# Attention groups of a two-block transformer: one pipeline slot in another order

## The reference

```python
# block 1 (_mixing): three kinds of heads
oa = _dsa(qa, ka, va, qi, ki, wi)       # 4 heads, top-128 keys of an index score
ob = _stick_breaking(qb, kb, vb)        # 4 heads
oc = _swa_sinks(qc, kc, vc, sinks)      # 8 heads, window of 128 keys, a sink each
o = jnp.concatenate([oa, ob, oc], axis=2)
o = _rms(o, g_out).reshape(B, L, MIX_WIDTH)      # root mean square of each head's output
return o @ w_o
...
# block 2 (_hybrid_mixer)
p = _masked_softmax(s1, mask) - lam * _masked_softmax(s2, mask)   # _diff_attention, 4 heads
...
o = _rmsnorm(o, subln_g, SUBLN_EPS) * (1.0 - lambda_init)
...
p = _masked_softmax(sc, _chunk_mask(start, s))   # _mla, 4 heads, no norm behind it
...
return jnp.concatenate([y_a, y_b, y_c], axis=-1) @ w_out          # y_c: a state space scan
```

## Time and profile before

| | |
|---|---|
| median of 3 runs | 3133.03 us (3124.57 to 3137.35) |
| the profiled execution | 3130.37 us, span 3128.6 us, mean granted clock of PE 0.951 |
| PE busy in the span | 2908.3 us (93%) |
| DVE busy | 1787.2 us (57%) |
| ACT busy | 756.2 us (24%) |
| POOL busy | 931.1 us (30%) |

### The profile page before, as it was taken

How to read it: one execution, slowest core, us unless ns; L and a number is a source line. 1 busy time by engine, 2 the same in 40 slices (tenths; PEclk the granted TensorE clock), 3 DMA queues, 4 the chain that set the end, 5 groups by cost and what they waited for, 6 DMA issues and landing times.

```text
span 3128.6 us, 33693 instructions
## 1 busy us (share of the span) xinstructions
PE 2908.3 (93%) x12126; PEld 2133.1 (68%) x12126; DVE 1787.2 (57%) x3803; ACT 756.2 (24%) x1781; POOL 931.1 (30%) x794
## 2 busy tenths in 40 slices
PE   8888999999997899999989988999999998899997
PEld 4354688888544578888854456888884454688886
DVE  2673469388367447938854545877824634551433
ACT  2354310000235431000022353201112335320111
POOL 0301224443330124444412202344440400344442
PEclk9989999999998799999989988999999998899998
DMA  6115034244221013434421101254421210122221
GB/s 256 64 61 215 28 138 166 101 148 170 91 80 61 1 55 121 175 108 156 154 76 56 61 27 68 108 183 186 156 100 57 59 50 23 40 94 96 81 81 54
DMA packets 45412, 313.28 MB, mean 100 GB/s; under 512 B 5424, under 2 KB 5552, under 8 KB 31040
## 3 DMA queue, kind: packets, MB, share of 16 engines
q1 hardware_dynamic: 42912, 306.88, 27.0%
q10 hardware_dynamic: 2304, 4.20, 0.6%
q0 software_dynamic: 32, 0.07, 0.0%
HBM read 298.53 MB, written 2.10 MB: 96 GB/s over the span
## 4 chain that ended last, share of the span: by engine, by line
PE 70%; DVE 18%; ACT 6%; issue 3%; DMA 1%; POOL 1%; DVEq 0%; SPq 0%; ACTq 0%; POOLq 0%
PE bank L1114 39%; PE bank L1094 9%; PE bank L1440 7%; PE bank L1168 3%; DVE nw L2067 3%; PE bank L1264 2%; DVE sel L2304 2%; DVE m L2303 1%; PE bank L1307 1%; DVE SPT L2368 1%; ACT SPT L1756 1%; PE bank L1294 1%; PE bank L1229 1%; PE bank L1567 1%; DMA sel<-in_mod_pieces 1%
## 5 line engine op out<-in xcount | busy, mean ns | idle before, releaser
L1000 POOL TENSOR_TENSOR SPT<-ring 128x512 f32<-128x512 f32 (+2 forms) x140 | 175.2, 1252 | 956.3 <-DMA ring<-in_slabs 493.0
L1114 PE MATMUL bank<-U,ring 128*128 128x256 f32 x1728 | 412.2, 384 | 10.8 <-DVE U L2101 10.5
L1114 PEld LDWEIGHTS bank<-U,ring 128*128 128x128 f32 x1728 | 332.8, 193 | 58.4 <-DVE U L2101 12.5
L2067 DVE SCALAR_TENSOR_TENSOR nw<-sel,c,nw 128x256 f32<-128x256 f32 x504 | 321.7, 638 | 31.2 <-DMA sel<-in_mod_pieces 13.5
L1114 PE MATMUL bank<-U,SPT 128*128 128x256 f32 x1296 | 312.5, 381 | 3.0 <-POOL SPT L1005 3.0
L1114 PEld LDWEIGHTS bank<-U,SPT 128*128 128x128 f32 x1296 | 247.4, 191 | 37.7 <-POOL SPT L1005 4.4
L1114 PE MATMUL bank<-hT,SPT 128*128 128x256 f32 x1088 | 257.1, 379 | 0.0
L1440 PE MATMUL bank<-hT,ring 128*128 128x512 f32 x544 | 249.7, 607 | 7.1 <-ACT hT L1873 7.1
L2127 DVE TENSOR_TENSOR rb<-bank,nw 128x256 f32<-128x256 f32 x108 | 45.5, 422 | 355.9 <-PE bank L1114 259.1
L1114 PE MATMUL bank<-hT,ring 128*128 128x256 f32 x1088 | 246.1, 379 | 0.0
L1114 PEld LDWEIGHTS bank<-hT,ring 128*128 128x128 f32 x1088 | 207.0, 190 | 28.0 <-DMA ring<-in_slabs 0.3
(11 more groups left out here) (344 smaller groups left out, 4501.9 us busy)
## 6 DMA issues: line engine op xcount, KB each, us to landing
ring<-in_slabs SPq DMA_DIRECT2D x86, 2048.0 KB, 8.0
sel<-in_mod_pieces SPq DMA_DIRECT2D x144, 512.0 KB, 4.5
ring<-in_slabs SPq DMA_DIRECT2D x8, 1536.0 KB, 7.0
ring<-in_slabs SPq DMA_DIRECT2D x8, 1280.0 KB, 8.3
tab<-U SPq DMA_DIRECT2D x40, 128.0 KB, 2.0
U<-in_slabs SPq DMA_DIRECT2D x2, 2048.0 KB, 22.5
tmp<-nw ACTq DMA_DIRECT2D x16, 256.0 KB, 2.9
ring<-in_slabs SPq DMA_DIRECT2D x2, 1808.0 KB, 11.7
```

Source lines behind the costliest of these rows:

```text
L1000: pool.tensor_tensor(e1, a21, a22, ALU.add).then_inc(*pool_order.up())
L1114: mm = pe.matmul(into[j][:, c:c + HALF], lhs[:, k, :], rhs[:, k, :], start=(begin and k == 0), stop=(end and k == kp - 1))
L2067: ins = dve.scalar_tensor_tensor(a, w[:, k, :], c[:, j:j + 1], a, ALU.mult, ALU.add)
```

## The change

Both functions that make the slots are rewritten. A slot has five groups in flight in place of four, and there is one slot more for each stream. The old step `pv` is split: PE's and ACT's part keeps the name, DVE's becomes `rd`. The old step `on` is split: ACT's part (logarithm and exponent) becomes `ln`, DVE's keeps the name. In a slot j the order is now: early `ot` of j-4, `pv` of j-2, `ln` of j-3, `sc` of j; late `cb` of j-1 (d only), `rd` of j-2, `on` of j-3, `tp` of j-1. Before, it was: early `on` of j-3, `cb` of j-1, `sc` of j; late `pv` of j-2, `tp` of j-1, `ot` of j-3. Since the statistics of a group now live one slot longer, DVE's `sc` waits for the scaling of the group four before it. The bounds of the streams in `woven` stay as they are.

```diff
 def group_slots(groups):
     out = []
-    for j in range(len(groups) + 3):
-        early, late = [], []
-        if 0 <= j - 3 < len(groups):
-            early.append(("on", groups[j - 3]))
-        if j < len(groups):
-            early.append(("sc", groups[j]))
-        if 0 <= j - 2 < len(groups):
-            late.append(("pv", groups[j - 2]))
-        if 0 <= j - 1 < len(groups):
-            late.append(("tp", groups[j - 1]))
-        if 0 <= j - 3 < len(groups):
-            late.append(("ot", groups[j - 3]))
+    for j in range(len(groups) + 4):
+        back = {d: groups[j - d] for d in range(5) if 0 <= j - d < len(groups)}
+        early = [(kind, back[d]) for kind, d in (("ot", 4), ("pv", 2), ("ln", 3), ("sc", 0)) if d in back]
+        late = [(kind, back[d]) for kind, d in (("rd", 2), ("on", 3), ("tp", 1)) if d in back]
         out += [early, late]
     return out
...
 def group_slots2(groups):
...
-        if 0 <= j - 3 < len(groups):
-            early.append(("on", groups[j - 3]))
-        if 0 <= j - 1 < len(groups) and GROUPS2[groups[j - 1]][0] == "d":
-            early.append(("cb", groups[j - 1]))
-        if j < len(groups):
-            early.append(("sc", groups[j]))
...
+        early = [(kind, back[d]) for kind, d in (("ot", 4), ("pv", 2), ("ln", 3), ("sc", 0))
+                 if d in back and (kind != "ot" or back[d] in TURNS2)]
+        late = [(kind, back[d]) for kind, d in (("cb", 1), ("rd", 2), ("on", 3), ("tp", 1))
+                if d in back and (kind != "cb" or GROUPS2[back[d]][0] == "d")]
         out.append([early, late])
...
# ScalarE, both blocks
-                    elif kind == "on":
+                    elif kind == "ln":
...
# VectorE, step "sc", both blocks (s2 in block 2)
+                        if g >= 4:
+                            dve.wait_ge(*s1["un"].after(l, g - 3))
...
# VectorE, both blocks
-                    elif kind == "pv":
+                    elif kind == "rd":
```

More of the change, by code:

```diff
@@ L1957, in _ @@
                                            ACT.Square).then_inc(*s2["uq"].up())
-                    elif kind == "on" and GROUPS2[st[1]][0] == "d":
+                    elif kind == "ln" and GROUPS2[st[1]][0] == "d":
                         g = st[1]
@@ L2539, in _ @@
                         stat = statD[:, g % 4, :]
+                        if g >= 4:
+                            dve.wait_ge(*s2["un"].after(l, g - 3))
                         if g >= 2:
```

## The result

The kernel after takes 3214.55 us (median of 4 runs, 3211.34 to 3216.06) against 3133.92 for the one before (4 runs, 3124.57 to 3137.35): a ratio of 1.0261, 95% interval 1.0237 to 1.0285. It is slower by 81 us, where 47 were forecast, and 2.5 us above the range. The profiled execution took 3211.34 us, its span is 3209.5, 80.9 more than before.

What follows compares the result with a forecast made beforehand. PE was taken to bound most of the kernel, a DVE-ACT ring its c and d stretches. 2 x (7 + 17) = +48 on the profiled 3130.4 us gave the forecast of 3180, range 3140 to 3212.

Steps and rivals of the forecast that it cites:

- c, +7 a layer: Block 1's eight window groups: new rings through PE, longer start and end; +7 us a layer (-1 to +11).
- The steady four slots: Block 1, masks 3 to masks 7, the larger ring in each slot: 32.6 us, +0.8 (low -1.5, high +2).
- pv's ring: Block 1: scores, masks, exponents, copies, pv, next scores in series, 8.4 us a full group; through ot's scaling 8.7.
- d, +17 a layer: Block 2's twelve differential groups: scores behind copies, turned weights behind cb; +8.8 to +22.3 us, nearer the upper end.
- the +1.2 for sc 6: Start of d: the scores of group 6 come behind pv 4 on PE, +1.2 us.
- First slots: d, masks 6 to 11: ring of masks, exponents, copies, pv, scores; 29.7 to 36.0 us, +1.4 to +7.7.
- Slots with output projections: d, masks 11 to 17: projections ahead of scores in four slots cover nothing; 43.6 to 49.5 us, +5.4 to +11.3.
- a, 0 a layer: Six sparse groups: other matmuls between scores and pv cover the ring; nothing, or -4 to +4 without that cover.
- m, and sc 6: MLA groups: key projections about as long as the ring, 0 to +1 us; scores 6 behind pv 4, +1.2.
- The added waits, 0: DVE's scores waiting for earlier scaled outputs, 20 in block 1, 28 in block 2: costed at nothing, 7.7 us at most.
- The worse one: Clock lower through most of d, c at its upper bounds: d +28, c +11, twice, 3208 us; chance 0.15.
- The faster one: In c and d, copies and masks come early enough that PE no longer waits; half its idle saved, 3105 us; chance 0.12.

Runs made afterwards that it cites:

- moving ot: Changed kernel with ot(j-4) issued behind the scores of j instead of ahead of pv(j-2), both blocks: 3214.21 us, ratio 1.0260.
- The two moves: Changed kernel with PE's scores issued ahead of ot and pv, and cb(j-1) ahead of the masks in block 2: alone 3142.31 and 3176.74 us, together 3109.24.
- the old order: Changed kernel's split steps in the instruction order and slot count of the kernel before, keeping only the 48 added DVE waits: 3132.16 us, ratio 0.9995.
- the later top-k rounds: Kernel with PE's scores first and cb ahead of the masks, block 1's top-k stream ending at 1.3 instead of 1.15: 3121.58 us, ratio 0.9950.
- `wo` early: Kernel with PE's scores first and cb ahead of the masks, first-half output projections spread from the third d slot instead of the sixth: 3128.28 us.

## Why the prediction came out as it did

**The direction, the order and most of the signs held.** c and d are longer, d by more; the squares' waits are nearly gone; PE's waits at pv for yB and at tp for cb are 13.3 + 10.8 + 51.4 = 75.5 us, "some 50 us or more" (27.5 before); the clock in d is 0.73, below 0.86. Of the signs of being wrong, c below 70 (taken as there, from its first masks, it was 80.7 and 83.7) and the first d slots below 28 did not come. The third, that pv finds its copies ready, was too coarse: PE waits for them in 24 of 64 pv steps, and where the wait at ot or the one for cb was taken away, the wait at pv grew (10.8 to 23.1 and 13.3 to 26.4 us above).

**c, +7 a layer: right.** Measured +6.2 and +9.2. The steady four slots are 33.2 and 34.2 (32.6 said; 31.8 before), the start +1.2 and +3.1 (+2.4 said), the end 21.17 against 17.58, +3.6 as said. In the second layer the four slots' +2.5 is above their high bound of 2. That pv's ring alone would hold c as long as ot's did was in the sum, and moving ot showed it.

**The step that failed: d, +17 a layer (8.8 to 22.3).** Measured +31.3 and +31.8, with each of its three parts above its own upper bound. (As I divide the span, the +1.2 for sc 6 falls into m; without it the forecast was +16, 7.6 to 21.1.) The mechanism, a ring through PE and cb's wait, was right; what was too small is this term. Masks 6 to 11 were to take 29.7 to 36.0 and took 40.3; masks 11 to 17, 43.6 to 49.5, took 53.0; the end, 17.0 to 18.3 less 1.8, took 18.9.

*First slots.* My ring (masks, exponents, copies, pv, scores) had 8.2 us for 256 keys at the lower clock, and with cb ahead of the masks that interval does take 8.17. The change has 8.75, since cb and tp stand in the ring in place of the exponents: tp can't run before cb, and cb is behind the masks. The sum is further off than that, and the first interval shows where: masks 6 to 7 take 8.76 against 4.34 before, because pv 5 of the last m group, 16 matmuls, stands ahead of scores 7, waits for its copies and then runs at the lower clock (3.45 us, 1.97 before):

```profile
1838.12 3.45 PE L1524 MATMUL bank<-VT,yB 128*128 128x64 f32 x16 [1.95 <-ACT yB L1926]
```

*Slots with output projections.* I priced cb's place at 2.6 to 3 us in four slots. The price held, 2.61 and 3.01, but PE waits for it in five (I left out tp 12, whose slot has no projection at all), and in three of these slots it waits for copies at pv as well (0.72 to 0.84). Of the projections behind the five waits one takes 3.60, the others 4.92 to 6.20, where the price at the lower clock was 5.74. Timeline of PE in the kernel after, tp 12 and tp 15 with the `wo` that follows each:

```profile
1896.00 0.53 PE L1510 MATMUL bank<-cst,SPT 128*128 128x128 f32 x3 [2.61 <-DVE SPT L2573]
...
1900.71 4.92 PE L1078 MATMUL bank<-U,ring 128*128 128x512 f32 x8
...
1918.75 1.09 PE L1510 MATMUL bank<-cst,SPT 128*128 128x128 f32 x4 [3.01 <-DVE SPT L2573]
1919.62 5.61 PE L1078 MATMUL bank<-U,ring 128*128 128x512 f32 x8
```

At full clock a `wo` takes 3.60. And I priced the first slots by pv's ring alone and the later ones by cb's wait alone. The two moves show that the later slots pay for both (12.3 and 5.6 in the table): with cb ahead d falls by 19, with the scores first by 19 to 20, with both by 38. My expectation for the kernel with cb ahead made the same mistake again, 8 to 15 us where 38 came.

**a, 0 a layer: right within the spread.** Measured +5.8 and -0.6, the first above its bound of 4; the old order has +4.5 and -4.1 with the same order of instructions. With PE's scores first a takes 249.3 in all, before 248.9.

**m, and sc 6.** +1.9 a layer, where 0 to 1 and 1.2 were said. **The added waits, 0:** right.

**Rivals.** The worse one (3208) named the clock and c's upper bounds and was closest; it still had d at +28, and c at +11 where +6.2 and +9.2 came. The faster one failed as the change stands, and its mechanism is real: with both moves 3109, which its working put at 3105. That the two numbers lie so close is in part luck: the rival took half of its gain from c, which gives 1.1 of it. The condition named for it, copies done before PE reaches pv, is what the two moves come nearer to: PE's wait for them in block 2 is 7.5 us, against 13.3 after (7.6 before). The Trainium skill ("Perfetto Trace Analysis", Optimizing Scalar/DVE Operations) says that where Scalar and Vector aren't saturated but cause bubbles on other engines, breaking up their instructions may let the work finish sooner; the change breaks up no instruction, it only moves them, so no run here shows that.

What stays open: how much of the first slots' 12 us is the clock. The first interval lies ahead of the added matmuls, and these may cost time themselves, so I take the 4.4 us as a lower bound; that is argued, not shown. The longer end of c, some 4 us a layer, is in the best kernel too, and the later top-k rounds took only 1 of it back.

## What to carry to other kernels

When a step moves ahead on one engine, write down for each engine what stands behind it in the queue, and walk the ring round once: here the step that was meant to free DVE put PE's scores behind ACT's copies. Two costs in the same slots, here a wait and a ring, are to be added unless one of them is shown to hide the other. The idea of a slower change can be sound: two moves of one step each turned 81 us lost into 22 won.

## What the hardware showed that I had not expected

Matmuls that compute nothing, put where PE waited, shortened the stretch they stood in: 39.32 to 35.66 us, with the granted clock at 0.86 in place of 0.56. The other way round, a higher clock bought nothing where the added dense work (`wo` early, clock 0.83 in place of 0.63) stood in front of what the other engines wait for.
